# Gate matmuls of a recurrent branch as three fp32r products of high and low parts

## The reference

```python
xc = causal_depthwise_conv(x_lru, conv_w[l], conv_b[l])          # 4 taps
xb = xc.reshape(B, S, LRU_BLOCKS, LRU_BLOCK)                      # 8 blocks of 128 channels
r  = sigmoid(einsum('bsnc,ncd->bsnd', xb, w_r) + b_r)             # gate 1: per block 128 x 128
gi = sigmoid(einsum('bsnc,ncd->bsnd', xb, w_i) + b_i)             # gate 2
log_a = -LRU_C * r * softplus(-lam_param)
a = exp(log_a)
bterm = sqrt(max(-expm1(2.0 * log_a), 0)) * gi * xc
_, h = associative_scan(_lin_combine, (a, bterm), axis=1)         # h[t] = a[t] * h[t-1] + bterm[t]
y_lru = h * silu(g_lru)
```

## Time and profile before

| | |
|---|---|
| median of 3 runs | 3342.87 us (3342.13 to 3344.57) |
| span of the profiled execution | 3339.8 us |
| own time of the profiled execution, outside its span | not given apart; the median is 3.1 us above the span |
| PE busy | 3236.2 us, 97% |
| DVE, ACT, POOL busy | 44%, 26%, 35% |
| recurrent branch, about | 45 to 248 us of the span |

### The profile page before, as it was taken

How to read it: one execution, slowest core, us unless ns; L and a number is a source line. 1 busy time by engine, 2 the same in 40 slices (tenths; PEclk the granted TensorE clock), 3 DMA queues, 4 the chain that set the end, 5 groups by cost and what they waited for, 6 DMA issues and landing times.

```text
span 3339.8 us, 39742 instructions
## 1 busy us (share of the span) xinstructions
PE 3236.2 (97%) x15586; PEld 2682.9 (80%) x15586; DVE 1466.1 (44%) x2210; ACT 864.1 (26%) x1410; POOL 1154.4 (35%) x880
## 2 busy tenths in 40 slices
PE   6999999998999899999999999999999999999999
PEld 4778888887787677888888888888788878888887
DVE  6775666566445875543211332325314651313131
ACT  3545444444222231300223223201101210101020
POOL 2342122211366321223222222344335763434352
PEclk9999999999999999999999999999999999999999
DMA  3221001000243220144222122421113221111112
GB/s 134 95 73 44 26 26 39 27 31 26 76 145 120 66 87 32 51 161 155 63 61 67 56 72 64 131 66 51 51 45 120 95 82 45 51 49 47 51 46 81
DMA packets 92210, 234.25 MB, mean 70 GB/s; under 512 B 7680, under 2 KB 33920, under 8 KB 91920
## 3 DMA queue, kind: packets, MB, share of 16 engines
q1 hardware_dynamic: 53504, 186.67, 17.2%
q10 hardware_dynamic: 38544, 45.24, 4.3%
HBM read 212.84 MB, written 19.04 MB: 69 GB/s over the span
## 4 chain that ended last, share of the span: by engine, by line
PE 90%; DVE 7%; ACT 2%; issue 1%; DMA 0%; ACTq 0%; DVEq 0%
PE proj_bank L226 23%; PE proj_bank L228 23%; PE proj_bank L227 23%; PE aux_banks L226 2%; PE aux_banks L227 2%; PE aux_banks L228 2%; PE aux_banks L799 2%; PE aux_banks L880 2%; PE aux_banks L806 1%; PE aux_banks L2223 1%; PE aux_banks L1791 1%; PE aux_banks L2251 1%; PE aux_banks L587 1%; DVE aux_banks L1672 1%; PE aux_banks L2272 1%
## 5 line engine op out<-in xcount | busy, mean ns | idle before, releaser
L226 PE MATMUL proj_bank<-h_hi,slab_hi 128*128 128x512 f32 x2816 | 1120.6, 398 | 18.5 <-DVE h_lo L414 8.6
L228 PE MATMUL proj_bank<-h_hi,slab_lo 128*128 128x512 f32 x2816 | 1102.6, 392 | 0.0
L227 PE MATMUL proj_bank<-h_lo,slab_hi 128*128 128x512 f32 x2816 | 1101.4, 391 | 0.0
L247 POOL CAST slab_hi<-slab_raw 128x1024 fp32r<-128x1024 f32 x292 | 311.4, 1066 | 2140.1 <-PE proj_bank L228 1634.4
L251 POOL TENSOR_TENSOR slab_lo<-slab_raw,slab_hi 128x512 fp32r<-128x512 f32 x584 | 843.2, 1465 | 23.4
L226 PEld LDWEIGHTS proj_bank<-h_hi,slab_hi 128*128 128x128 f32 x2816 | 532.1, 189 | 138.0 <-issue 11.1
L228 PEld LDWEIGHTS proj_bank<-h_hi,slab_lo 128*128 128x128 f32 x2816 | 531.5, 189 | 113.7
L227 PEld LDWEIGHTS proj_bank<-h_lo,slab_hi 128*128 128x128 f32 x2816 | 532.7, 189 | 107.9 <-issue 2.2
L226 PE MATMUL proj_bank<-ffn_hi,slab_hi 128*128 128x512 f32 x512 | 199.2, 389 | 0.4 <-issue 0.4
L227 PE MATMUL proj_bank<-ffn_lo,slab_hi 128*128 128x512 f32 x512 | 199.2, 389 | 0.0
L228 PE MATMUL proj_bank<-ffn_hi,slab_lo 128*128 128x512 f32 x512 | 199.2, 389 | 0.0
(11 more groups left out here) (380 smaller groups left out, 4183.1 us busy)
## 6 DMA issues: line engine op xcount, KB each, us to landing
slab_raw<-wts SPq DMA_DIRECT2D x292, 512.0 KB, 3.5
ada_w<-ada_w SPq DMA_DIRECT2D x40, 384.0 KB, 3.2
ada_w_early<-ada_w SPq DMA_DIRECT2D x24, 384.0 KB, 3.5
ssd_decay_rows<-decay_sums ACTq DMA_DIRECT2D x16, 512.0 KB, 3.9
dil_rows<-dilated_out ACTq DMA_DIRECT2D x12, 520.0 KB, 7.7
x_first<-xT SPq DMA_DIRECT2D x4, 1024.0 KB, 9.2
x<-xT ACTq DMA_DIRECT2D x4, 1024.0 KB, 6.6
x_kept<-x ACTq DMA_DIRECT2D x16, 256.0 KB, 2.7
```

What stands on the lines that cost most here:

```text
L226: pe.matmul(bank, k.whi[:, slot, wk, :], hi[:, xk, cols], start=first and a == 0, stop=False)
L227: pe.matmul(bank, k.whi[:, slot, wk, :], lo[:, xk, cols], start=False, stop=False)
L228: mm = pe.matmul(bank, k.wlo[:, slot, wk, :], hi[:, xk, cols], start=False, stop=last and a == len(ks) - 1)
L247: pool.tensor_copy(k.whi[:, to], k.raw[:, slot]).then_inc(k.s_hi, 1)
```

## The change

The gates are computed as the projections are: from high and low parts in fp32r.

- ACT copies all gate weights (128x2048) into `gate_w_hi`, once, after `silu(0)`; DVE subtracts to make `gate_w_lo`, once, after `conv(0)`.
- In each iteration ACT makes `lru_conv_hi` from `lru_conv` (`conv_high(n)`), after `silu(n)` and before `root(n-1)`. DVE makes `lru_conv_lo` (`conv_low(n)`), after `recurrence(n-1)` and before the modulation half. Both tiles are single buffers, so both wait for `gates(n-1)`.
- PE's `gates(n)` now waits for `conv_low(n)` instead of `conv(n)` and issues twelve matmuls instead of four.

```diff
+    gwhi, gwlo = (k.at(f"gate_w_{n}", k.Y + 8 * i, [P, LRU_BLOCKS, 2, P], F32R) for i, n in enumerate(("hi", "lo")))
+    xchi, xclo = (k.at(f"lru_conv_{n}", k.Y + 16 + 4 * i, [P, T], F32R) for i, n in enumerate(("hi", "lo")))
+    s_high, s_low = k.sem("lru_gate_high"), k.sem("lru_gate_low")
...
         def gates(n):
 
             if n == 0:
-                pe.wait_ge(s_gw, 16)
-            pe.wait_ge(s_conv, n + 1)
+                pe.wait_ge(s_low, 1)
+            pe.wait_ge(s_low, n + 2)
             if n:
                 pe.wait_ge(s_sig, n)
             for i in range(2):
                 for c in range(2):
-                    mm = pe.matmul(k.aux[:, 2 * i + c, :], gw[:, n, i, :], xc[:, n % 2, c * HALF:(c + 1) * HALF], start=True, stop=True)
+                    out, cols = k.aux[:, 2 * i + c, :], slice(c * HALF, (c + 1) * HALF)
+                    pe.matmul(out, gwhi[:, n, i, :], xchi[:, cols], start=True, stop=False)
+                    pe.matmul(out, gwhi[:, n, i, :], xclo[:, cols], start=False, stop=False)
+                    mm = pe.matmul(out, gwlo[:, n, i, :], xchi[:, cols], start=False, stop=True)
             mm.then_inc(s_gates, 1)
...
+        def conv_high(n):
+            if n:
+                act.wait_ge(s_gates, n)
+            act.wait_ge(s_conv, n + 1)
+            act.activation(xchi[:], xc[:, n % 2], ACT.Copy).then_inc(s_high, 1)
...
             silu(n)
+            if n == 0:
+                act.wait_ge(s_gw, 16)
+                act.activation(gwhi[:], gw[:], ACT.Copy).then_inc(s_high, 1)
+            conv_high(n)
             if n:
                 root(n - 1)
...
+        def conv_low(n):
+            if n:
+                dve.wait_ge(s_gates, n)
+            dve.wait_ge(s_high, n + 2)
+            dve.tensor_tensor(xclo[:], xc[:, n % 2], xchi[:].bitcast(F32), ALU.subtract).then_inc(s_low, 1)
...
             conv(n)
+            if n == 0:
+                dve.wait_ge(s_high, 1)
+                dve.tensor_tensor(gwlo[:], gw[:], gwhi[:].bitcast(F32), ALU.subtract).then_inc(s_low, 1)
             if n in (3, 5, 7):
                 modulation_columns(k, dve, (n - 3) // 2)
             if n:
                 recurrence(n - 1)
+            conv_low(n)
             if n < EARLY_HALVES:
```

More of the change, by code:

```diff
@@ L572, in lru_stage @@
     k.banks_read = (s_evac, 2 * LRU_SLABS + EV)
-    k.spent += [s_evac, s_conv, s_gates, s_sig, s_au, s_m2, s_mult, s_y, s_gw, s_lam]
+    k.spent += [s_high, s_low, s_evac, s_conv, s_gates, s_sig, s_au, s_m2, s_mult, s_y, s_gw, s_lam]
     LAST = LRU_BLOCKS - 1
```

## The result

The changed kernel took 3353.57 us (median of 6 runs, 3349.85 to 3355.34) beside 3344.09 for the kernel before on the same chip (6 runs, 3342.13 to 3344.57): ratio 1.003, 95% interval 1.0019 to 1.0042. Slower by 9.5 us, where 3345.1 and a range up to 3349.5 were forecast. The profiled execution has a span of 3351.1 us and an own time of 3352.89.

The account below looks back on a forecast made before the run. PE, busy 199.71 of 200 us in the recurrent branch, was taken as the bound. Gains of -5.0 at seven gates and +7.2 at the branch's end made +2.2 on 3342.87: 3345.1 us, range 3341.0 to 3349.5.

Parts of the forecast that it names:

- the gain on PE: Gates 0 to 6: twelve fp32r matmuls take 2.72 us where the plain ones took 3.44, 0.71 less a block.
- the last wait and its price: At gates(7): PE waits 10.3 us for conv_low(7), low clock follows; first small attention matmuls (L806) come 7.2 us late.
- wait for the bank: End of the branch: PE's 2.78 us wait for L647, and 1.7 us from the low clock behind it, would be gone.
- Margin 3: ACT's next copy: conv(2) ends by 114.9 at most, ACT asks at 115.0; a slip moves only a root with slack.
- the term of -5.0: Recurrent loop: gates 0 to 6 each gain 0.71 us, 5.0 us together, if nothing comes to wait.
- Block 0: Weight copy at most 2.1 us, its subtraction at most 2.4, conv_low(0) done at 71.0, against the gates at 75.35.
- margin 2: The x slab two blocks on, behind the modulation steps: of 3.2 us of room, 0.2 to 0.8 is left.
- Margin 1: Gates of an odd block: conv_low ready 0 to 0.5 us ahead; no wait taken, otherwise up to 0.5 each.
- Rival B: The loop through DVE and SP becomes the bound; PE waits before x slabs and odd gates, 3351 to 3353 us; 9%.

Follow-up runs that it names:

- e3: Changed kernel with conv_low made for block 0 only, the other blocks using that stale low part: 3338.42 us, ratio 0.9988 to the kernel before.
- e5: Changed kernel with POOL's subtraction for the silu slabs of blocks 1 to 7 cut to 1/64 of its columns: 3345.0 us, ratio 1.0009 to the kernel before.
- a0: The changed kernel run again without any edit: 3353.82 us, ratio 1.0036 to the kernel before.
- e4: Changed kernel with conv_high moved between ACT's two silu evacuations and conv_low behind L688 (block 7 slightly earlier): 3343.62 us, ratio 1.0006 to the kernel before.
- e6: Changed kernel with only conv_low moved, behind L688 of the recurrence in every block: 3344.31 us, ratio 1.0004 to the kernel before.
- e2: Changed kernel with block 7 without copies, its gates four plain 32-bit matmuls again: 3345.93 us, ratio 1.0009 to the kernel before.
- e10: Changed kernel with both copies moved as in e4, the convolution's first tap on ACT (blocks 1 to 7), block 7's gates plain: 3338.78 us, ratio 0.999.
- e9: Kernel before the change, with the convolution's first tap moved from DVE to ACT in blocks 1 to 7: 3342.2 us, ratio 1.0001 to the kernel before.

## Why the prediction was wrong

**Right: the gain on PE.** 3.44 us became 2.72, and where nothing waits (e3, e5) the last silu comes at 239.62 and 239.67, against 240.35 forecast; about 0.6 of the difference is that these executions reached the first gates that much earlier than the one before.

**Right: the last wait and its price.** 10.31 us against 10.3. The clock behind it, by window of the kernel after (as the earlier trace rows):

```profile
250.80:257.30 6.50, 0.00 (x0) 0.00 (x0) 6.41 (x4) 1.02 (x1) 0.74 (x1) 0.50 0.27 81
257.40:262.90 5.50, 5.33 (x12) 3.79 (x12) 0.00 (x0) 0.30 (x2) 0.00 (x0) 0.54 0.00 0
263.00:268.00 5.00, 5.00 (x22) 4.17 (x23) 0.00 (x0) 4.97 (x5) 0.00 (x0) 1.00 0.00 0
```

A granted clock of 0.50, which is 1.2 GHz, is there already while PE stands; the twelve matmuls took from 257.39 to 262.7, 5.3 us, and from 263.00 the clock is 1.00, 2.4 GHz. No wait for the bank was left. (The wait of 9.75 us that this price was read from the earlier trace rows is not PE's longest, as I called it: at the start of the program PE waits 19.3 us. Nothing hangs on that.) From the last silu to L832 it took 38.03 us; forecast were 283.3 - 245.32 = 38.0. That they agree to 0.1 us is luck beyond the mechanism: in the second execution (a0), after the same wait of 10.31, the clock was back at 1.00 about 3.3 us behind the first gate matmul (256.26) instead of 5.1, and L832 followed the last silu by 37.24.

**Wrong: Margin 3.** "It just holds, and a slip moves only a root that has its own slack against the gates of an even block" is the step that failed, and with it the term of -5.0 in the sum. The copy itself did hold (it waited for the convolution 0.15 and 0.43 us, in iterations 5 and 6 only); the slip did not stop at the root. I priced all of DVE's rows as they stood before, 1.21 to 1.23 for L670 to L672, and let only their starts move. But in iteration 3 those three ended 0.4 us ahead of POOL's cast, in the others only the last one or two lay beside it, and the two moved toward each other. Once beside it they took up to 2.32 each, and it was not the root's slack that went but DVE's own: from 112.5 us to the end of `conv_low(6)` at 232.8 DVE never waited for a root. The sum of an iteration was never made (spare 2.1; asked 1.85, or 3.5 with the overlap); the margins were taken one by one, for one block, and slips do not come back in a queue without idle time. By the Trainium skill ("SBUF — State Buffer", section "SBUF: two separate sides"), such operations lock each other out; the trace agrees. In iteration 3 the two engines take turns: POOL's first half ended at about 141.24 + 2.19 = 143.43, and L688, which was issued at 142.16, ended at 144.47, the 1.22 us that it takes alone behind 143.25. None waited for a whole instruction of the other (1.22 became 2.31, halves of 1.27 became 2.19), since each was issued while the other's was already under way. I used that page for `conv_low` and the scan, and not for the operations that the change only displaces.

**Block 0 and margin 2** held: the weight copy took 1.91 us, its subtraction 2.29, gates 0 to 2 came free of waits (in a0 gates 2 waited 0.16), and no x slab was waited for. **Margin 1** held for block 1, for which it was worked out, and not for the later odd blocks: gates 3 and 5 waited 1.73 and 2.30, where "up to 0.5" was allowed. **Rival B** named 3351 to 3353 and a full loop, but through SP and the x slabs; that path is seen only in e4 and e6, where DVE's order was changed. The measured path is DVE's own queue.

**The size.** Forecast of the loop -5.0, measured +1.5: 6.5 us apart. 6.0 are idle time, and about 0.3 more goes at each of four waits (gates 3 take 154.33 - 151.48 = 2.85 instead of 2.72, and the matmul ahead drains 0.39 instead of 0.23), less a start of the branch that lay about 1 us earlier; some 0.3 stay unaccounted for. With 8.75 at the merge, the span is 11.3 longer in these two executions and the medians 9.5 apart. The start of the same POOL cast is 8.7 us later at 443 us as at the merge, so the last 2.6 arise far behind the change. Time at the low clock, added up over windows of 1 us, is 64.8 us in the execution before and 78.5 after, but 3.4 and 13.6 of that lie ahead of 300 us; behind it stand 61.4 and 64.9. 3.4 us more at half the clock would be, by my estimate, 1.7 of the 2.6; why two executions differ there was not tried.

## What to carry to other kernels

Before adding work to an engine, add up its idle time over one whole iteration, without waits that stay anyway, and subtract the new work, the shorter period and every operation that the shift may push beside another engine's; margins of single waits don't show it. An engine made faster pulls forward what it releases: in iteration 3 DVE's trio came 1.3 us later and POOL's slab 2.8 us earlier, and operations that had just missed each other overlapped almost throughout. And look at the last pass of a loop by itself: there the split saved 0.7 us and cost 7.3, and leaving it out (e2) brought all of that back. The largest single repair of a complete kernel was a matter of place: `conv_low` moved to where DVE had waited (e6) took 9.5 us off, in the loop and at the end.

## What was not expected of the hardware

- The same wait was not always followed by the same clock. Before, 2.78 us of waiting for the bank was followed by 3.4 us at 0.50; in e10 a wait of 2.79 was followed by none, although another of 0.59 came 6 us later. e9 (2.80) and e2 (2.81) went as the kernel before. Busy time by window of e10:

```profile
258.20:263.00 4.80, 4.80 (x21) 3.99 (x22) 4.77 (x3) 4.19 (x5) 2.84 (x2) 1.00 0.14 34
263.00:268.00 5.00, 4.41 (x20) 3.33 (x19) 4.12 (x5) 1.92 (x3) 0.00 (x0) 1.00 0.19 72
```

From that wait to the merge e10 took 270.08 - 258.18 = 11.90 us and the kernel before 276.09 - 263.44 = 12.65: 0.75 us of e10's lead that its edit doesn't explain, and that need not be there in every execution.

- An operation on POOL slows beside DVE as much as DVE does: halves of the split take 1.27 us alone and 2.19 with a two-input operation of DVE beside them, and casts 1.04 and 2.12. In the kernel after POOL stood idle for 13 us and more before every x slab from 100 to 240 us, so only DVE's side counted.
